# Where VectorE does the far-key sums and the first output block in the attention stage of a hybrid decoder layer

## What is computed

```python
A_GROUPS = ((128, 1), (512, 4), (2048, 16))
for g, (w, d) in enumerate(A_GROUPS):
    nk = w // d + 1
    dist = jnp.arange(nk) * d
    s = einsum('bqhd,bqkhd->bhqk', qblk[:, :, g], kg) * scale - slopes[g] * dist
    lse = logsumexp(s, axis=-1);  p = exp(s - lse[..., None])
    outs.append(einsum('bhqk,bqkhd->bqhd', p, vg));  lses.append(lse)
wts = softmax(stack(lses, axis=0), axis=0)
o = einsum('gbhq,gbqhd->bqhd', wts, stack(outs, axis=0))
...
y_a = (silu(za) * o_a) @ w_pa
y_b = (silu(zr) * o_r) @ w_pb
```

## Time and profile before

| | |
|---|---|
| median of 3 runs | 983.08 us (980.69 to 986.93) |
| profiled execution | 980.83 us, span 979.1 us |
| PE busy | 928.5 us, 95% |
| PEld busy | 860.0 us, 88% |
| DVE busy | 557.0 us, 57% |
| ACT busy | 338.6 us, 35% |
| POOL busy | 204.9 us, 21% |
| mean granted TensorE clock | 0.986 |
| far sums (L1558) | 32, of 1.21 us each |
| PE's share of the chain that ended last | 75%; DVE 12%, DMA 4%, issue 4% |

### The profile page before, as it was taken

The page is one execution under the profiler, slowest core; times in us unless marked ns, Lnnn a source line. Parts: engine busy times, 40 slices in busy tenths (PEclk is TensorE's granted clock), DMA queues, the critical chain, the costliest instruction groups (busy, mean ns, idle before and its releaser), DMA issues.

```text
span 979.1 us, 19790 instructions
## 1 busy us (share of the span) xinstructions
PE 928.5 (95%) x7032; PEld 860.0 (88%) x7032; DVE 557.0 (57%) x1020; ACT 338.6 (35%) x518; POOL 204.9 (21%) x171
## 2 busy tenths in 40 slices
PE   5999999999999999999999999999879999999994
PEld 4999999899989998997887877877649999999894
DVE  4347633763386338656777786786775333333348
ACT  4123312431243124243443453443454433333110
POOL 0027102710271027151133123123110000000004
PEclk9999999999999999999999999999979999999997
DMA  8995599459945994262963783783765878876993
GB/s 271 223 270 199 182 184 315 152 169 188 311 158 163 198 317 150 76 237 100 320 230 117 260 294 120 250 314 111 247 259 192 288 256 273 278 249 243 323 368 122
DMA packets 162514, 219.73 MB, mean 224 GB/s; under 512 B 8336, under 2 KB 136080, under 8 KB 160656
## 3 DMA queue, kind: packets, MB, share of 16 engines
q1 hardware_dynamic: 157776, 205.90, 68.2%
q0 software_dynamic: 4048, 11.02, 3.5%
q10 hardware_dynamic: 656, 2.36, 0.7%
HBM read 206.53 MB, written 100.01 MB: 313 GB/s over the span
## 4 chain that ended last, share of the span: by engine, by line
PE 75%; DVE 12%; DMA 4%; issue 4%; ACT 2%; SPq 0%; DVEq 0%; POOL 0%; POOLq 0%; ACTq 0%
PE bank L734 17%; PE bank L736 17%; PE bank L735 17%; PE bank L1013 6%; PE bank L729 4%; PE bank L764 3%; PE bank L846 2%; DVE wl L1427 2%; PE bank L1058 2%; DVE part_l L1649 1%; PE bank L1049 1%; DVE scoresp L1502 1%; DVE fsum L1558 1%; DMA cslot<-in_cache_kv_w_dram 1%; PE bank L974 1%
## 5 line engine op out<-in xcount | busy, mean ns | idle before, releaser
L734 PE MATMUL bank<-xh,wh 128*128 128x288 f32 x640 | 192.2, 300 | 3.2 <-DVE vn L1491 2.9
L734 PE MATMUL bank<-wh,xh 128*128 128x256 f32 x640 | 186.6, 292 | 3.5 <-DVE wl L1427 3.0
L736 PE MATMUL bank<-xh,wl 128*128 128x288 f32 x640 | 189.2, 296 | 0.0
L735 PE MATMUL bank<-xl,wh 128*128 128x288 f32 x640 | 189.1, 295 | 0.0
L735 PE MATMUL bank<-wl,xh 128*128 128x256 f32 x640 | 182.0, 284 | 0.0
L736 PE MATMUL bank<-wh,xl 128*128 128x256 f32 x640 | 181.9, 284 | 0.0
L1427 DVE TENSOR_TENSOR wl<-raw,wh 128x1024 fp32r<-128x1024 f32 (+1 forms) x104 | 128.4, 1269 | 50.1 <-ACT wh L1201 40.0
L1201 ACT ACTIVATE wh<-raw 128x1024 fp32r<-128x1024 f32 (+1 forms) x104 | 101.9, 1018 | 85.1 <-PE bank L764 41.4
L734 PEld LDWEIGHTS bank<-wh,xh 128*128 128x128 f32 x640 | 123.7, 193 | 6.1 <-issue 3.4
L734 PEld LDWEIGHTS bank<-xh,wh 128*128 128x128 f32 x640 | 120.8, 189 | 6.9 <-DVE vn L1491 6.2
L735 PEld LDWEIGHTS bank<-wl,xh 128*128 128x128 f32 x640 | 123.8, 193 | 1.2
(11 more groups left out here) (213 smaller groups left out, 1759.9 us busy)
## 6 DMA issues: line engine op xcount, KB each, us to landing
raw<-in_w_in_dram SPq DMA_DIRECT2D x128, 256.0 KB
cslot<-in_cache_kv_w_dram SPq DMA_DIRECT2D x32, 1024.0 KB, 6.3
out_dram<-in_cache_kv_w_dram SPq DMA_DIRECT2D x32, 1020.0 KB, 10.1
out_dram<-in_cache_kv_w_dram SPq DMA_DIRECT2D x12, 2040.0 KB, 10.2
far<-in_cache_kv_w_dram SPq DMA_DIRECT2D x32, 512.0 KB, 10.4
raw<-in_w_in_dram SPq DMA_DIRECT2D x16, 512.0 KB
out_dram<-in_cache_kv_w_dram SPq DMA_DIRECT2D x3, 2720.0 KB, 18.6
out_dram<-in_cache_kv_w_dram SPq DMA_DIRECT2D x16, 504.0 KB, 4.9
```

The costliest lines, as they stand in the source:

```text
L734: pe.matmul(out, lhs[0](k), rhs[0](k), start=(k == 0), stop=False)
L735: pe.matmul(out, lhs[0](k), rhs[1](k), start=False, stop=False)
L736: last = pe.matmul(out, lhs[1](k), rhs[0](k), start=False, stop=(k == n - 1))
```

## The change

Only VectorE's list inside `attention_head` is reordered; nothing is added or left out. Far sum 2 goes behind `values(21)` and `probs(1, 5)`, `values(22)` ahead of far sum 3, `output(0)` ahead of `zr(0)`; far sums 4, 5, 6 and 7 each go to a later place, the last one behind the two final multiplications.

```diff
                 values(20)
                 softmax(2)
-                far_sum(2)
                 values(21)
                 probs(1, 5)
+                far_sum(2)
+                values(22)
                 far_sum(3)
-                values(22)
                 softmax(3)
-                far_sum(4)
+                output(0)
                 zr(0)
-                output(0)
                 probs(2, 7)
                 output(1)
-                far_sum(5)
+                far_sum(4)
                 low(c + 6, 0)
                 zr(1)
                 probs(3, 9)
-                far_sum(6)
                 output(2)
                 probs(3, 11)
                 zr(2)
-                far_sum(7)
+                far_sum(5)
                 output(3)
+                far_sum(6)
                 zr(3)
                 for n in range(2):
                     b = group(12 + n)
                     o = oa[:, bass.ds(h * NTOK + (NS + 2 * n * P), 2 * P)]
                     tt(o, b[:, 0:2 * P], o, ALU.mult).then_inc(tg_free[n % 2], 1)
+                far_sum(7)
```

## The result

The changed kernel takes 991.25 us (median of 18 runs, 984.71 to 997.28) against 982.07 us (18 runs) before: ratio 1.0089, 95% interval 1.0069 to 1.011, so 8.7 us slower by the ratio (6.8 to 10.8); the plain medians lie 9.2 us apart. The forecast was 989.5 us, range 984.0 to 996.0. The profiled execution took 984.71 us, the fastest of the 18, with a span of 983.0 us, only 3.9 us above that of before.

What follows compares the result with a forecast made beforehand. TensorE, busy for 95% of the span, was taken as the bound, so VectorE edits count only through its waits. Waits of +4.5 us and clock of +3.0 us made +7.5 us, forecast 989.5 us, range 984.0 to 996.0.

Steps and rivals of the forecast that it cites:

- (a): values(22) ahead of far sum 3 releases TensorE's wait for vn earlier: gain 0.94 us a head.
- (b): output(0) ahead of far sum 4 and zr(0) leaves TensorE no wait for on: gain 0.7 us a head.
- (c): Far sums 4 to 7 each move later on VectorE, costing nothing until the last zr.
- (d): Far sum 7 at the head's end exposes its store before kv_out: 2.8 us stall, net +1.2 us at three borders.
- (e): Fourth border, where all engines meet at a_end: +0.9 us, TensorE's stall growing from 0.56 to some 3.2 us.
- (f): New border stalls bring TensorE's clock down: 1.5 us each, counted at two of the four, +3.0 us.
- rival 2: Handshake exposed at the borders but the clock holds: +4.5 us, 985.3 to 987.6; chance 0.19.
- (3): Store at the borders lands in 3.4 to 4.0 us, stalls of 4.7 us: +16, 997 to 999; chance 0.10.
- (4): TensorE's waits for vn and on stay, another release being behind them: +11, 992 to 994; chance 0.08.
- (5): Faster: the store's handshake is hidden at the head's start, −6.6 us, 974 to 976.5; chance 0.05.

Runs made afterwards that it cites:

- experiment 1: The changed kernel with far sum 7 ahead of the last gating, zr(3), instead of at the head's end: 974.83 us, ratio 0.9923 to the kernel before.
- experiment 11: Repeat of the changed kernel with POOL giving kv_out ahead of the store of fsum: 979.68 us, ratio 0.9974 to the kernel before.
- experiments 10: The kernel of experiment 1 with 3.7 us of products on POOL ahead of its part of a_end: 979.88 us, ratio 0.9975 to the kernel before.
- 9: The kernel of experiment 1 with three reductions into an unread tile on VectorE behind a_end: 980.76 us, ratio 0.9994 to the kernel before.
- experiments 6: The changed kernel with 12 unused matmuls of 256 columns ahead of each head's third unit: 991.82 us, ratio 1.0089 to the kernel before.

## Why the prediction was right

**(a) and (b), the gains.** Together 1.74 us a head against 1.65 predicted. The working treated them as two terms that add, and that is wrong for (a) by itself: since softmax 3 keeps its time, as the prediction says, `on` keeps its time as well, and TensorE, through unit 23 earlier, only waits longer in front of it. In the sum it did no harm, because (b) releases `on` early enough for both.

**(c)** cost nothing, as said: experiment 1 has the sums 4 to 6 in their new places and gains all.

**(d), the handshake.** The store was issued 0.74 us after the sum and landed 1.7 us later, and the stall was 2.74 to 2.76 us against 2.8 predicted, +1.27 us a head net of the gain against +1.2. The steps from landing to VectorE were 0.4 instead of 0.3 us. The choice of 1.7 us for the landing, out of 1.7 to 4.0, carried this, and all four stores of the changed kernel landed in 1.7, in both profiles. The 2.0 us that the prediction cites from the Trainium skill, "DMA: Bandwidth & Descriptors", section "Anatomy of one DMA", would have been 0.3 us too long at each.

**(e)** The stall at the end of the stage is 3.42 us against 3.2.

**(f), the clock.** Counted at the borders of stage A, over the profiles of all kernels with such stalls there:

| TensorE idle at the border | clock fell behind it |
|---|---|
| 1.3 us (with the twelve matmuls) | 0 of 3 |
| 2.75 us (changed, changed again, last sum alone moved) | 5 of 9 |
| 3.1 to 3.5 us (fourth border) | 7 of 8 |
| 3.9 and 4.5 us (last sum twice) | 4 of 4 |

A head with a fall takes 100.05, 100.21 or 100.07 us, one without 98.71: 1.3 to 1.5 us for a fall, as priced. The changed kernel had one fall of four in its first profile and three of four in its second, two of four on the mean, the number the forecast took. The forecast did not work that number out; it was a choice between none and all, and that it was met is in part luck. At the fourth border the term was set too low: a fall came in 7 of 8 and took between 1.4 and 3.0 us of full rate from the restart on, some 2 us on the mean. With these counts, which come from the same runs and so are no test, the sum is 3 × 1.27 + 1.1 for the stalls (3.42 − 0.57 = 2.85 at the fourth border, less 1.74), 3 × 5/9 × 1.4 = 2.3 and 7/8 × 2 = 1.8 for the clock, 9.0 in all, against 8.7 measured and 7.5 forecast. The forecast's base, 989.5 − 7.5 = 982.0 us, was a choice as well, between the profile's time and the median of three; the median of 18 is 982.07.

The prediction charges all four stalls by the Trainium skill, "TensorE: Matmul & The Clock Gate", section "Why this matters for your kernels". That rule is for idle gaps above a certain length, which the prediction leaves out, so this was more than the rule says; of the stalls of 2.75 us, 5 of 9 brought the clock down.

Nor is the table a rule of the stall's length. The prediction says that the trace before shows nothing between 1.6 and 4 us, and that is a misreading: TensorE waits 2.97 us before 20.55 and 2.34 us before 925.30, with the clock at 1.00 behind both. Both speak for rival 2. All fourteen profiles have the wait of 2.97 us, and the clock fell behind it in eight of them. Ahead of `qdup` in the first head TensorE waits up to 3.63 us (experiment 1; 2.96 in experiment 11), and there the clock fell in none. The wait of 2.97 us in the kernel before and behind it in the changed one, then the one for `qdup` in experiment 1:

```profile
20.55 0.58 PE L734 MATMUL bank<-wh,xh 128*128 128x256 f32 x1 [2.97 <-DVE wl L1427]
20.00:22.00 2.00, 1.46 (x7) 1.46 (x8) 0.86 (x2) 1.50 (x2) 0.00 (x0) 1.00 0.08 19
...
22.00:24.00 2.00, 2.00 (x11) 2.00 (x11) 0.85 (x1) 0.00 (x0) 0.00 (x0) 0.50 1.33 410
...
74.46 0.33 PE L729 MATMUL bank<-con,qdup 128*128 128x128 f32 x1 [3.63 <-DVE qt L1464]
74.00:76.00 2.00, 1.54 (x12) 1.54 (x13) 0.69 (x3) 1.16 (x2) 0.65 (x1) 1.00 0.75 185
```

What besides the length decides is not shown by these runs.

**The 3.9 us of the first profile.** At TensorE's restart in stage B this execution is 425.45 − 419.51 = 5.94 us behind the one of before, near the 3 × 1.27 + 1.1 + 1.34 = 6.3 us of three borders, the fourth and one fall. Further on the gap is 4.59 us:

```profile
507.92 0.27 PE L974 MATMUL bank<-part_h,qm 128*64 128x128 f32 x1 [1.16 <-DVE part_l L1649]
...
512.51 0.28 PE L974 MATMUL bank<-part_h,qm 128*64 128x128 f32 x1 [1.16 <-DVE part_l L1649]
```

Between the two the clock fell in the profile of before (0.64 in 476 to 478, 0.51 in 478 to 480) and not in this one. The remaining 0.7 us are not traced to a place.

**The rivals.** That the clock holds (2) is refuted by the falls in both profiles, that the landing is slow (3) by the rows of both, that the waits stay (4) by the table of waits. The side of faster (5) was real but needed another place for the sum: experiment 1.

**Open.** The kernel with `kv_out` given early gained 0.6 and 2.6 us in two measurements where 2.5 to 4 was expected, and the kernels with a stall at the fourth border alone lost 1 and 3 us more than stall and one average fall, which the intervals don't tell from nothing. Longer half clock behind that border covers some 1.5 us of it in the traces of experiments 10 and 11, none in that of 9. The rest isn't traced to a place. The clock also falls at varying places later in stage B (around 433, 476, 505, 550, 590 or 671 us, once or more in some executions and not at all in others), and the first head has a wait of 0 to 3.6 us for `qdup`, ahead of every changed instruction, in all kernels: both are spread of single executions, and no single profile can give a difference of 2 us.

## What to carry to other kernels

Where work is moved to the end of a loop body, look at what is handed over after it: not the work (1.21 us here) but the issue of the store, its landing and the semaphores that come behind it (0.74 + 1.7 + 0.4 = 2.8 us), and at the first instruction of the next turn that stands behind that handover. Put it into the last place where the engine waits anyway that still leaves room for the handover; here three instructions earlier made 991 us into 975. A stall of 2.75 us or more at these borders cost more than its length, and did so in some executions only, so a profile with few falls of the clock flatters the kernel.

## What was not expected of the hardware

Removing one wait of TensorE gave exactly nothing (97.46 against 97.44 us a head) while the next one stood. The same stall of 2.75 us, at the same border of the same kernel, took the clock down in one execution and not in another: at the second border in the second profile, not in the first. A wait of 3.63 us in the first head of experiment 1 did not take it down at all. After stalls of 3.2 to 3.5 us at the fourth border half clock lasted 5 to 6 us from the restart in three executions (experiments 6, 10 and 11) although TensorE was fully busy from the restart on.
